# One diffusion-backbone step on one core: branch B projected into turned queries and keys, expert outputs gathered plainly and added by VectorE

## The chip, the core and the metric

The kernel runs on one core of a Trainium2 chip. The metric is the device time of one execution in microseconds (us). The engines are TensorE (PE in the profile; its weight loads PEld), VectorE (DVE), ScalarE (ACT), GpSimd (POOL) and SyncE (SP), which only issues transfers. A trailing q (ACTq) is an engine's queue: issues, loads of registers, waits.

## The reference

Two layers run over 640 tokens of width 1024: 512 latent tokens and 128 context tokens, all in f32. Per layer:

```
mod = silu(cond) @ w_mod + b_mod                # shift, scale, gate, twice
h   = x * (1 + sc1) + sh1
qa,ka,va, qb,kb,vb, qc,kc,vc = split(h @ w_in)  # branches A, B, C
y   = (ga*(oa@w_br0) + gb*(ob@w_br1) + gc*(oc@w_br2)) @ w_o
x   = layernorm(alpha*x + g1*y)
m   = top-2 of 16 experts on x*(1+sc2)+sh2, each (silu(h@w1)*(h@w3))@w2
x   = layernorm(alpha*x + g2*m)
```

Branch A is differential attention with rotary positions, B is neighbourhood attention (8 heads, no rotary positions and no norm of queries and keys, window bias), C is grouped-query attention with normed queries and keys. Latent tokens also read cached context keys and values. The context tokens' new keys and values are outputs too.

## The kernel before, in words

Tokens lie in five tiles of 128 (`NT = 5`, the last is the context). The weights are one wall of 1 MB pieces in device memory; SyncE streams them in order into a ring of six slots (`load`, L602) and waits for a slot to be freed by TensorE or VectorE. Each f32 matmul is two instructions on TensorE in the trace.

Each layer is one block, with a program for each engine. It goes through the branches A, B, C: `project(br)`, `attend(br)`, `merge(br)`. `PU` lists the projection's units: (branch, chunk of 512 columns of `w_in`, token tile). A unit is eight matmuls with `hT` (the modulated input, features on partitions) as the stationary operand and 512 columns of the ring as the moving one (L808, through the helper `mm`), into one of four PSUM banks. ScalarE copies the unit to `tok` (L1371); TensorE turns it, four transposes against the identity one unit later (`transpose_unit`, L883); ScalarE copies the result into `QT` (scaled, L1335) or `KT` (L1337). This holds for branch B's query and key chunks 3 and 4 also, ten units. Chunk 5 holds B's values and is not turned. In branch B's projections VectorE sums sixteen modulation pieces from the ring (L1660, L1662); TensorE adds them over the partitions at the places that `MOD_SUMS` names, behind unit (4, 0) and unit (5, 3) (`sum_partials`, L835). GpSimd stores new keys from `tok` and waits for the store, then the values, and prepares B's bias.

Gates of the merge are computed by `fill`: units of eight matmuls with the ring's weights as the stationary operand and 320 columns of `hT` as the moving one. Eight of these matmuls stand ahead of the last transposes of branch A, the rest between the parts of the attention.

The experts: for each of 17 blocks of 128 tokens GpSimd gathers token rows (`gather`, L742), TensorE turns them and multiplies with w1, w3, w2. ScalarE takes the latent gate row times a flag (`slot_gate`, L559); VectorE, once w2's result is ready, adds the context part (L563) and multiplies the result by the token's weight and the gate row (L564). Both are in `gate_output`, called by `keep_output`. ScalarE stores the block's rows (L1487). At the end of the layer's block ScalarE waits for its stores. Then every engine loads a count (L2018), meets the others at a barrier (L2019), and the next block begins.

```
for t in range(4):
    fetch_outputs(pool, t)      # two gathers a tile: L537 adds into x, L538 writes Y2
scale_power(pool, ch, 0)
fetch_outputs(pool, 4)
```

`fetch_and_scale` runs on GpSimd at the start of layer 1 and in the final block. The first gather accumulates in the transfer (`compute_op=ALU.add`) into `x`, which already holds the scaled residual. VectorE adds `Y2` and takes statistics (`add_outputs`, L551, L494 to L499), GpSimd raises the variance to the power -0.5 (`scale_power`, L504), VectorE makes the negated mean (L1528), ScalarE normalises (L1299) and TensorE turns the tile (L853). The final block does the same with sums (L2141, L2142), squares by ScalarE (L2129), variance (L2147), centring times the gain (L2151) and scaling plus offset (L2153); SyncE loads gain and offset rows `rowsF` (1 MB) at the start of this block and stores each finished tile.

## Time and profile before

| what | us |
|---|---|
| median of 3 runs (lowest, highest) | 2271.79 (2268.26, 2272.42) |
| the profiled execution | 2269.82 |
| its span, first to last instruction | 2267.7 |
| TensorE busy | 2115.3 |
| VectorE busy | 1083.0 |
| ScalarE, GpSimd busy | 519.6, 236.7 |

The mean granted clock of TensorE is 0.971 of full speed. Busy time is not the bound by itself: what matters is who waits at each place. In a timeline a row gives start, duration, engine, line, operation, output and inputs, the count of merged instructions, and in brackets the idle time before it with what ended it. Matmuls are pipelined and their ends modelled: the pace of a run is read from the start of a row to the start of the next one.

### The profile page before, as it was taken

Reading aid. Unit: us, or ns where it says so; the run is one execution under the profiler, and the core shown is the slowest. Engines: PE = TensorE matmul, PEld = TensorE weight load, DVE = VectorE, ACT = ScalarE, POOL = GpSimd, SP = SyncE. Lnnn points to the kernel's source line nnn. Section 1 sums busy time; section 2 is a strip of 40 time slices with the busy share of each in tenths; the row PEclk is TensorE's granted clock in tenths of the full one; section 3 lists DMA queues with packets and bytes.
Section 4 is the critical chain, followed back from the end, with each engine's and each line's share of the span. In section 5 each row is a group of like instructions: output and inputs, shape, how many; then the busy total and the mean of one; then the engine's idle time right before and its main releaser. Section 6 shows DMA issues by size and latency. Waiting matters only on the chain. (4 is left out here: it accounts for less than half of the span.)

```text
span 2267.7 us, 26885 instructions
## 1 busy us (share of the span) xinstructions
PE 2115.3 (93%) x10730; PEld 1376.2 (61%) x10730; DVE 1083.0 (48%) x1701; ACT 519.6 (23%) x992; POOL 236.7 (10%) x272
## 2 busy tenths in 40 slices
PE   6999999999999998899689999999999999969991
PEld 3457754576567654788544676447756775458880
DVE  1135457243444364664242453745434444865434
ACT  2014301242134200122130341113402440012221
POOL 1000010020100000211110001002101000011113
PEclk8999999999999999899899999999999999979996
DMA  8121166311110325899760111642111105159985
GB/s 335 44 78 38 48 217 227 112 52 60 56 40 32 159 104 222 293 370 359 259 221 37 61 38 61 223 172 82 45 60 58 38 20 232 40 188 361 362 323 176
DMA packets 59439, 334.64 MB, mean 148 GB/s; under 512 B 8704, under 2 KB 9696, under 8 KB 30192
## 3 DMA queue, kind: packets, MB, share of 16 engines
q1 hardware_dynamic: 33408, 238.70, 29.0%
q0 software_dynamic: 15008, 56.96, 7.6%
q10 hardware_dynamic: 10896, 37.23, 4.2%
q8 instruction: 87, 1.43, 0.3%
q14 instruction: 40, 0.33, 0.0%
HBM read 300.47 MB, written 35.01 MB: 148 GB/s over the span
## 5 line engine op out<-in xcount | busy, mean ns | idle before, releaser
L808 PE MATMUL ps<-ring,hT 128*128 128x512 f32 (+1 forms) x1280 | 530.5, 570 | 1.9 <-issue 1.9
L808 PE MATMUL ps<-hT,ring 128*128 128x320 f32 x1536 | 464.3, 440 | 0.0
L808 PEld LDWEIGHTS ps<-ring,hT 128*128 128x128 f32 x1280 | 239.8, 191 | 253.6 <-issue 246.8
L808 PEld LDWEIGHTS ps<-hT,ring 128*128 128x128 f32 x1536 | 272.8, 190 | 97.3 <-issue 1.6
L808 PEld LDWEIGHTS ps<-zT,ring 128*128 128x128 f32 x2176 | 254.1, 194 | 18.4 <-issue 15.3
L808 PE MATMUL ps<-zT,ring 128*128 128x128 f32 x2176 | 258.5, 278 | 2.3 <-ACT zT L1483 2.3
L808 PE MATMUL ps<-R,ring 128*128 128x512 f32 (+1 forms) x768 | 211.1, 435 | 4.6 <-DVE zT L1795 3.2
L1430 ACT COPY R<-ps 128x512 f32<-128x512 f32 (+2 forms) x170 | 96.2, 566 | 383.8 <-PE ps L1021 381.6
L808 PEld LDWEIGHTS ps<-R,ring 128*128 128x128 f32 x768 | 116.9, 191 | 98.6 <-issue 92.5
L808 PE MATMUL ps<-ring,zT 128*128 128x512 f32 x320 | 139.0, 593 | 0.0
L1662 DVE SCALAR_TENSOR_TENSOR R<-ring,cs,R 128x2048 f32<-128x2048 f32 x56 | 131.7, 2352 | 5.8 <-DMA ring<-in_wall 4.0
L960 PE MATMUL ps<-R 64*128 64x128 f32 (+2 forms) x992 | 123.2, 374 | 7.0 <-ACT R L1337 3.5
L808 PE MATMUL ps<-ring,R 128*128 128x512 f32 x272 | 122.5, 593 | 3.1 <-issue 3.1
L1725 DVE RECIPROCAL rinv<-rsum 128x2 f32<-128x2 f32 x96 | 15.9, 166 | 218.4 <-ACT R L1416 218.4
L960 PEld LDWEIGHTS ps<-R 64*128 64x128 f32 x992 | 92.1, 186 | 37.9 <-issue 12.2
L563 DVE SCALAR_TENSOR_TENSOR R<-R 128x1024 f32<-128x1024 f32 x34 | 43.7, 1285 | 142.8 <-PE ps L808 142.8
L1695 DVE TENSOR_REDUCE nmax<-ps 128x2 f32<-128x1280 f32 x64 | 95.5, 1492 | 28.6 <-PE ps L960 27.8
L808 PEld LDWEIGHTS ps<-ring,zT 128*128 128x128 f32 x320 | 60.2, 190 | 72.7 <-issue 72.2
L1416 ACT ACTIVATE R<-ps,nmax 128x640 f32<-128x640 f32 x128 | 100.5, 790 | 2.5 <-DVE nmax L1695 0.5
L1371 ACT COPY R<-ps 128x512 f32<-128x512 f32 (+1 forms) x54 | 28.5, 527 | 309.4 <-PE ps L808 309.0
L1021 PEld LDWEIGHTS ps<-ident,R 128*128 128x128 f32 x648 | 76.9, 141 | 29.0 <-DVE R L1716 6.3
L1021 PE MATMUL ps<-ident,R 128*128 128x128 f32 x648 | 87.8, 273 | 6.1 <-DVE R L1716 4.3
(237 smaller groups left out, 1954.2 us busy)
## 6 DMA issues: line engine op xcount, KB each, us to landing
ring<-in_wall SPq DMA_DIRECT2D x224, 1024.0 KB
y_rows<-R ACTq DMA_DIRECT2D x34, 512.0 KB, 9.6
R<-in_rows POOLq DMA_DIRECT2D x2, 4096.0 KB, 15.3
R<-mrows POOLq DMA_DIRECT2D x16, 512.0 KB, 17.8
R<-in_x ACTq DMA_DIRECT2D x10, 512.0 KB, 8.5
h_rows<-R ACTq DMA_DIRECT2D x10, 512.0 KB, 2.7
R<-in_bias POOLq DMA_DIRECT2D x8, 384.0 KB, 4.1
x_state<-R POOLq DMA_DIRECT2D x1, 2560.0 KB, 9.8
```

The source lines that it names most:

```text
L563: ch.step(nc.vector.scalar_tensor_tensor(gsel[e % 2], G2[:, 1, :], in_ctx[:, 0, e:e + 1], gsel[e % 2], ALU.mult, ALU.add), v_chain)
L808: ins = nc.tensor.matmul(out, w, m, start=start, stop=stop, **kw)
L960: return nc.tensor.matmul(out, QT[lo:lo + 64, b, 128 * r:128 * r + 128], KT[lo:lo + 64, key_slot(br, b), k0:k0 + n], start=True, stop=True)
L1021: last = nc.tensor.transpose(ps[:, 3 + c + k // 4, 128 * (k % 4):128 * (k % 4) + 128], P[:, i % 2, c, 128 * k:128 * k + 128], ident[:])
L1371: ch.step(nc.scalar.copy(dst, src), a_copy)
L1416: ins = nc.scalar.activation(dst, src, ACT.Exp, bias=nmax[:, n + a:n + a + 1], accum_out=rsum[:, n + a:n + a + 1])
L1430: ch.step(nc.scalar.copy(dst, src), a_pt)
L1662: ins = V_.scalar_tensor_tensor(mod_acc[:, v], w, c, mod_acc[:, v], ALU.mult, ALU.add)
L1695: ch.step(V_.tensor_reduce(nmax[:, n:n + 2].unsqueeze(2), src, axis=AX.X, op=ALU.max, negate=True), v_max)
L1725: ch.step(V_.reciprocal(rinv[:, o:o + 2], rsum[:, n:n + 2]), v_rinv)
```

## The change

- Chunks 3 and 4 (queries and keys of branch B) are projected turned: eight units each instead of five (`turned`, `units`), with a 128-column slice of the ring as the stationary operand and 320 tokens of `hT` as the moving one. ScalarE copies the unit right into `QT` (scaled) or `KT`. Their transposes and second copies are gone; `QU` and `NEW_K` leave them out. The new keys are stored from `KT`, and the host turns the array. ScalarE waits for that store ahead of branch C. `MOD_SUMS` has (4, 1) for (4, 0).
- `gate_output` is split into `slot_gates` (L563's product, now ahead of the wait for w2's result) and `keep_gated`.
- `y_out` is cleared no more between blocks and counts over both layers (`stores`). ScalarE doesn't wait for the stores at the end of the block; GpSimd does, ahead of the gathers. Spare expert blocks use `extra_out`.
- Both outputs of a token are gathered plainly, into `Y1` and `Y2`; VectorE adds `Y1` (`first_outputs`).
- `rowsF` lies elsewhere and is loaded behind the last layer's weights. The final block sums two tiles ahead of the scaling.

```diff
@@ -53,7 +53,7 @@
 MOD_ORDER = ((2, 6, 0), (0, 0, 8))
-MOD_SUMS = ((4, 0), (5, 3))
+MOD_SUMS = ((4, 1), (5, 3))
 PROJECT_SLOTS = (0, 1, 2, 3, 4, 5) + 3 * (2, 3) + (0, 1) + 4 * (2, 3)
@@ -150,6 +150,11 @@
+def stores(layer, e, n):
+    return layer * len(range(n, NB, 2)) + len(range(n, e, 2))
 def near_values(r):
@@ -160,6 +165,16 @@
     return [*range(LAT), 5]
+def turned(c):
+    return c in (3, 4)
+def units(c):
+    return 8 if turned(c) else NT
@@ -292,11 +307,12 @@
+        Y1 = zf.rearrange("p (t n) -> p t n", t=NT)
         Y2 = area(8704, 5120).rearrange("p (t n) -> p t n", t=NT)
-        rowsF = area(0, 2048).rearrange("p (a n) -> p a n", a=2)
+        rowsF = area(24064, 2048).rearrange("p (a n) -> p a n", a=2)
@@ -308,6 +324,8 @@
         y_init = ctx.enter_context(nc.semaphore("output_rows_filled"))
+        y_out = [ctx.enter_context(nc.semaphore(f"expert_outputs_stored_{n}")) for n in range(2)]
+        last_rows_in = ctx.enter_context(nc.semaphore("last_rows_loaded"))
         full = [sem(f"piece_loaded_{s}") for s in range(SLOTS)]
@@ -533,12 +552,14 @@
-            first, second = (bass.IndirectOffsetOnAxis(ap=yrow[:, k, t:t + 1], axis=0) for k in range(2))
-            pool.indirect_dma_start(out=x[:, t, :], out_offset=None, in_=y_all, in_offset=first, compute_op=ALU.add).then_inc(yt_in[t], 16)
-            pool.indirect_dma_start(out=Y2[:, t, :], out_offset=None, in_=y_all, in_offset=second).then_inc(yt_in[t], 16)
-        def fetch_and_scale(pool, ch):
+            for k, Y in enumerate((Y1, Y2)):
+                pool.indirect_dma_start(out=Y[:, t, :], out_offset=None, in_=y_all,
+                                        in_offset=bass.IndirectOffsetOnAxis(ap=yrow[:, k, t:t + 1], axis=0)).then_inc(yt_in[t], 16)
+        def fetch_and_scale(pool, ch, layer):
+            for n in range(2):
+                pool.wait_ge(y_out[n], 16 * stores(layer, NB, n))
             for t in range(4):
@@ -546,6 +567,11 @@
+        def first_outputs(dve, ch, t):
+            dve.wait_ge(yt_in[t], 32)
+            ch.step(nc.vector.tensor_tensor(x[:, t, :], x[:, t, :], Y1[:, t, :], ALU.add), v_chain)
         def add_outputs(ch, t):
@@ -558,9 +584,12 @@
-        def gate_output(ch, e, w, s):
+        def slot_gates(ch, e):
             ch.step(nc.vector.scalar_tensor_tensor(gsel[e % 2], G2[:, 1, :], in_ctx[:, 0, e:e + 1], gsel[e % 2], ALU.mult, ALU.add), v_chain)
+        def keep_gated(ch, e, w, s):
             ch.step(nc.vector.scalar_tensor_tensor(ysb[:, e % 2, :], flat(4, 1024), w, gsel[e % 2], ALU.mult, ALU.mult), s)
@@ -614,6 +643,8 @@
                         load(i, layer, first + (MOE0 + n))
+                    if last_layer:
+                        sp.dma_start(rowsF[:], A["last_rows"]).then_inc(last_rows_in, 16)
                     if not last_layer:
@@ -688,7 +719,12 @@
                             typ = CHUNK_TYPE[c]
-                            if typ in ("k", "kv"):
+                            if typ == "k" and turned(c):
+                                pool.wait_ge(a_copy, AU.index(PU.index((br, c, units(c) - 1))) + 1)
+                                pool.dma_start(OUT["bk"][layer].rearrange("p (b t) -> p b t", b=4), KT[:, :, LTOK:TOK]).then_inc(new_k_out, 16)
+                                pool.wait_ge(new_k_out, 16 * (br + 1))
+                            elif typ in ("k", "kv"):
@@ -915,6 +951,11 @@
                                         wk = take("in").rearrange("p (k n) -> p k n", k=8)[:, k, :]
+                                    if turned(c):
+                                        b, part = divmod(t, 2)
+                                        last = mm(ps[:, bank_of(i), 0:320], wk[:, 128 * b:128 * b + 128], hT[:, k, 320 * part:320 * part + 320],
+                                                  k == 0, k == KB - 1, frees=k < KB - 1)
+                                        continue
                                     last = mm(ps[:, bank_of(i), 0:w], hT[:, k, 128 * t:128 * t + 128], wk, k == 0, k == KB - 1, frees=k < KB - 1)
@@ -963,7 +1004,7 @@
-                            pe.wait_ge(a_qk, 10 * (br + 1))
+                            pe.wait_ge(a_qk, 20 if br == 2 else 10)
                             pe.wait_ge(a_copy, len([a for a in AU if PU[a][0] <= br]))
@@ -1337,8 +1378,10 @@
                     def project(br):
+                        if br == 2:
+                            act.wait_ge(new_k_out, 32)
                         for c in CHUNKS[br]:
-                            for t in range(NT):
+                            for t in range(units(c)):
                                 i = PU.index((br, c, t))
@@ -1358,6 +1401,9 @@
                                         pass
+                                    elif turned(c):
+                                        b, part = divmod(t, 2)
+                                        dst, src = (QT if c == 3 else KT)[:, b, 320 * part:320 * part + 320], ps[:, bank_of(i), 0:320]
                                     elif CHUNK_TYPE[c] in ("v", "kv"):
@@ -1367,7 +1413,9 @@
                                         dst, src = tok[:, q % 2, :], ps[:, bank_of(i), :]
-                                    if c != 6:
+                                    if c == 3:
+                                        ch.step(nc.scalar.activation(dst, src, ACT.Copy, scale=HD ** -0.5), a_copy)
+                                    elif c != 6:
                                         ch.step(nc.scalar.copy(dst, src), a_copy)
@@ -1501,8 +1549,6 @@
                     store_output(NB - 1)
-                    for s in range(2):
-                        act.wait_ge(y_out[s], 16 * len(range(s, NB, 2)))
@@ -1558,10 +1604,11 @@
                         for t in range(NT + 1):
+                            if t < NT:
+                                first_outputs(dve, ch, t)
                             if t:
                             if t < NT:
-                                dve.wait_ge(yt_in[t], 32)
                                 add_outputs(ch, t)
@@ -1981,10 +2028,11 @@
                         dve.wait_ge(a_gsel, e + 1)
+                        slot_gates(ch, e)
                         dve.wait_ge(pe_e, e + 1)
-                        if e >= 2:
-                            dve.wait_ge(y_out[e % 2], 16 * (e // 2))
-                        gate_output(ch, e, slot_w[:, e, e:e + 1] if e < NE else extra_w[:, NE:NE + 1], v_y)
+                        if stores(layer, e, e % 2):
+                            dve.wait_ge(y_out[e % 2], 16 * stores(layer, e, e % 2))
+                        keep_gated(ch, e, slot_w[:, e, e:e + 1] if e < NE else extra_w[:, NE:NE + 1], v_y)
@@ -2137,7 +2186,7 @@
-                    dve.wait_ge(yt_in[t], 32)
+                    first_outputs(dve, ch, t)
                     ch.step(nc.vector.scalar_tensor_tensor(x[:, t, :], x[:, t, :], 1.0, Y2[:, t, :], ALU.mult, ALU.add, accum_out=lnst[:, t, 12:13]), v_chain)
@@ -2146,20 +2195,25 @@
+                def centred(t):
+                    ch.step(nc.vector.scalar_tensor_tensor(x[:, t, :], x[:, t, :], lnst[:, t, 14:15], rowsF[:, 0, :], ALU.add, ALU.mult), v_chain)
                 def scaled(t):
-                    ch.step(nc.vector.scalar_tensor_tensor(x[:, t, :], x[:, t, :], lnst[:, t, 14:15], rowsF[:, 0, :], ALU.add, ALU.mult), v_chain)
                     dve.wait_ge(g_rs, t + 1)
-                dve.wait_ge(rows_in, 16)
+                dve.wait_ge(last_rows_in, 16)
+                summed(0)
                 for t in range(NT):
-                    summed(t)
-                    if t:
-                        variance(t - 1)
-                        scaled(t - 1)
-                variance(NT - 1)
-                scaled(NT - 1)
+                    if t == 0:
+                        summed(1)
+                    variance(t)
+                    centred(t)
+                    if t + 2 < NT:
+                        summed(t + 2)
+                    scaled(t)
```

## Rows read from the trace of the kernel before

**Rows 1.** The page: busy time, share of the span, instructions.
```profile
PE 2115.3 (93%) x10730; PEld 1376.2 (61%) x10730; DVE 1083.0 (48%) x1701; ACT 519.6 (23%) x992; POOL 236.7 (10%) x272
```

**Rows 2.** Timeline, PE, projections of branch B, layer 0: start us, us, what.
```profile
340.90 7.03 PE L808 MATMUL ps<-ring,hT 128*128 128x512 f32 x16
347.77 0.60 PE L883 MATMUL ps<-ident,R 128*128 128x128 f32 x4
348.20 7.03 PE L808 MATMUL ps<-ring,hT 128*128 128x512 f32 x16
...
414.79 1.92 PE L835 MATMUL ps<-R 128*32 128x512 f32 x16
```

**Rows 3.** Timeline, PE: 320-column matmuls ahead of and inside the attention.
```profile
1253.73 4.47 PE L808 MATMUL ps<-hT,ring 128*128 128x320 f32 x16
1258.04 0.60 PE L883 MATMUL ps<-ident,R 128*128 128x128 f32 x4
...
426.95 3.50 PE L808 MATMUL ps<-hT,ring 128*128 128x320 f32 x12
430.38 0.92 PE L960 MATMUL ps<-R 64*128 64x256 f32 x8
```

**Rows 4.** Timeline, DVE: its last modulation sums, layer 0.
```profile
391.97 4.74 DVE L1662 SCALAR_TENSOR_TENSOR R<-ring,cs,R 128x2048 f32<-128x2048 f32 x2 [0.33 <-DMA ring<-in_wall]
```

**Rows 5.** Timeline, end of layer 0's experts: VectorE and ScalarE's queue.
```profile
1116.46 1.29 DVE L563 SCALAR_TENSOR_TENSOR R<-R 128x1024 f32<-128x1024 f32 x1 [3.58 <-PE ps L808]
...
1119.16 0.34 ACTq L1487 DMA_DIRECT2D y_rows<-R  x1
```

**Rows 6.** Line L2018, GpSimd's queue: duration ns, first and last start.
```profile
L2018 POOLq TENSOR_LOAD <-ovi x2: 320/410/499, 1122.2 to 2225.4; - x2
```

**Rows 7.** Busy time by windows: the engines, granted clock, DMA share, GB/s.
```profile
1120.00:1121.00 1.00, 0.00 (x0) 0.00 (x0) 0.00 (x0) 0.00 (x0) 0.00 (x0) 1.00 1.03 422
...
1132.00:1133.00 1.00, 0.00 (x0) 0.00 (x0) 0.00 (x0) 0.00 (x0) 0.69 (x2) 0.50 0.99 188
```

**Rows 8.** Timeline, POOL: gathers of tile 0 ahead of layer 1.
```profile
1124.74 1.58 POOL L537 DMA_INDIRECT R<-y_rows,yrow  x1 [35.26 <-issue]
1126.63 0.98 POOL L538 DMA_INDIRECT R<-y_rows,yrow  x1 [0.30 <-issue]
```

**Rows 9.** Line L538, the second outputs' gathers: issue to landing.
```profile
DMA to landing us min/median/max: 6.6/8.3/9.5
```

**Rows 10.** Line L742, the experts' token gathers: issue to landing.
```profile
DMA to landing us min/median/max: 5.7/8.9/9.8
```

**Rows 11.** Timeline, all engines: tile 0 ahead of layer 1.
```profile
1133.35 1.23 DVE L551 TENSOR_TENSOR R<-R 128x1024 f32<-128x1024 f32 x1 [7.02 <-DMA R<-y_rows,yrow]
...
1136.31 0.15 DVE L499 TENSOR_SCALAR small<-R 128x1 f32<-128x1 f32 x1
1137.29 0.59 POOL L504 TENSOR_TENSOR R<-small,half 128x1 f32<-128x1 f32 x1
...
1139.59 1.97 PE L853 MATMUL ps<-ident,R 128*128 128x128 f32 x8 [23.34 <-ACT R L1299]
```

**Rows 12.** Timeline, all engines: the final block.
```profile
2227.83 1.58 POOL L537 DMA_INDIRECT R<-y_rows,yrow  x1 [35.14 <-PEq L2107]
...
2237.52 1.23 DVE L2141 SCALAR_TENSOR_TENSOR R<-R 128x1024 f32<-128x1024 f32 x1 [15.24 <-DMA R<-y_rows,yrow]
...
2244.89 2.60 POOL L537 DMA_INDIRECT R<-y_rows,yrow  x1 [0.28 <-POOL R L504]
...
2253.63 1.57 POOL L504 TENSOR_TENSOR R<-small,half 128x1 f32<-128x1 f32 x1 [3.18 <-DVE small L2147]
...
2255.30 1.28 DVE L2153 SCALAR_TENSOR_TENSOR R<-R 128x1024 f32<-128x1024 f32 x1 [0.51 <-POOL R L504]
...
2260.06 1.28 DVE L2153 SCALAR_TENSOR_TENSOR R<-R 128x1024 f32<-128x1024 f32 x1 [0.51 <-POOL R L504]
...
2263.36 1.28 DVE L2153 SCALAR_TENSOR_TENSOR R<-R 128x1024 f32<-128x1024 f32 x1 [0.51 <-POOL R L504]
```

More of the change, by code:

```diff
@@ L376, in count @@
                 return self.n.get(s.num, 0)
-        PU = [(br, c, t) for br in range(3) for c in CHUNKS[br] for t in range(NT)]
+        PU = [(br, c, t) for br in range(3) for c in CHUNKS[br] for t in range(units(c))]
         def bank_of(i):
@@ L387, in out_bank @@
             return (i + 2) % 4
-        QU = [i for i, (br, c, t) in enumerate(PU) if CHUNK_TYPE[c] != "v"]
+        QU = [i for i, (br, c, t) in enumerate(PU) if CHUNK_TYPE[c] != "v" and not turned(c)]
         def by_dve(c, t):
@@ L402, in follows @@
             return i > 0 and i - 1 in QU and PU[i - 1][0] == br and i + 1 < len(PU)
-        NEW_K = [i for i, (br, c, t) in enumerate(PU) if t == CTX and CHUNK_TYPE[c] in ("k", "kv")]
+        NEW_K = [i for i, (br, c, t) in enumerate(PU) if t == CTX and CHUNK_TYPE[c] in ("k", "kv") and not turned(c)]
         def item(br, i):
@@ L637, in _ @@
                         pool.wait_ge(y_init, 16 * len(range(1, EXTRA, 4)))
-                        fetch_and_scale(pool, ch)
+                        fetch_and_scale(pool, ch, layer - 1)
                     def powers(dst, src):
@@ L698, in _ @@
                                 if typ == "k":
-                                    pool.dma_start(OUT[("ak", "bk")[br]][layer], tok[:, q % 2, 0:512]).then_inc(new_k_out, 16)
+                                    pool.dma_start(OUT["ak"][layer], tok[:, q % 2, 0:512]).then_inc(new_k_out, 16)
                                 else:
@@ L1339, in project @@
                     def project(br):
+                        if br == 2:
+                            act.wait_ge(new_k_out, 32)
                         for c in CHUNKS[br]:
-                            for t in range(NT):
+                            for t in range(units(c)):
                                 i = PU.index((br, c, t))
@@ L2078, in _ @@
                             act.wait_ge(v_y, 1)
[L2079 to L2080 removed]
+                            act.dma_start(A["y_rows"][NE + j], ysb[:, 0, :]).then_inc(extra_out, 16)
+                            act.wait_ge(extra_out, 16)
                         @block.vector
@@ L2099, in _ @@
                             dve.wait_ge(a_gsel, 1)
+                            slot_gates(ch, NE)
                             dve.wait_ge(pe_e, 1)
-                            gate_output(ch, NE, extra_w[:, NE:NE + 1], v_y)
+                            dve.wait_ge(y_out[NE % 2], 16 * stores(layer, NB, NE % 2))
+                            keep_gated(ch, NE, extra_w[:, NE:NE + 1], v_y)
                     nc.all_engine_barrier(sems_to_clear=all_sems)
@@ L2118, in _ @@
                 ch = Chain(pool)
-                fetch_and_scale(pool, ch)
+                fetch_and_scale(pool, ch, DEPTH - 1)
                 pool.dma_reset(all_sems)
```

8 lines of the change are left out of this document (3 added, 5 removed).

## The prediction

> **What bounds the kernel now.** I read the page first: TensorE is busy 93% of a span of 2267.7 us [rows 1]. So either its own work gets shorter or one of its pauses does; elsewhere nothing counts. Then TensorE's timeline through the projections of branch B, where the first part of the change lies. A unit is 16 instructions (8 f32 matmuls, two instructions each): they start at 340.90, the next instruction at 347.77, so a unit of 512 columns takes 6.87 us; the four transposes of the unit before take 0.43 us more, until 348.20 [rows 2]. No row there carries an idle time: the engine is the bound of this stage. VectorE sums the modulation pieces beside it and is done at 396.71, 18 us before TensorE asks for that sum at 414.79 [rows 2, 4].
>
> The second kind of place is where TensorE has nothing to do: between the last expert of layer 0 and layer 1 it is idle for 23.34 us, until 1139.59 [rows 11], and behind the last expert of layer 1 for good. In both pauses there is one chain: VectorE gates the last expert's output, ScalarE stores it, the block ends, GpSimd gathers, VectorE normalises. I read it in the timelines of these stretches [rows 5, 8, 11, 12].
>
> **Turned queries and keys.** Per layer, two chunks of 5 units go (10 x 6.87 = 68.7 us) and their 10 groups of transposes (10 x 0.43 = 4.3 us): 73.0 us. In come 2 x 8 units of 8 matmuls with 320 columns. The trace has just this unit in the fill behind branch A: 16 instructions from 1253.73 to 1258.04, 4.31 us [rows 3]. 16 x 4.31 = 69.0 us, so 4.1 us less per layer, 8.2 us in both. The columns are the same 5120; what is saved is the transposes. The upper bound of the price is the run of 12 such instructions between score tiles: 426.95 to 430.38, 3.43 us, 0.572 us per matmul [rows 3]. 128 x 0.572 = 73.2 us would give 0.2 us per layer back instead. I take 4.31, since its neighbours are 128-row work, as the new units' are; the 12 stand beside 64-row score tiles. ScalarE copies 16 times 320 columns in place of 20 times 512, so less than before: nothing. VectorE's first sum is now asked for behind 10 units of 4.31 (43.1 us from the chunk's start) instead of 6 x 6.87 + 5 x 0.43 (43.4 us): no new wait. The second comes 4.1 us sooner, against the 18 us of slack. The store of new keys moves to rows of the turned tile and GpSimd waits for it as before, one chunk ahead of anything due; nothing, by that cover. If the store were late, the next late thing would be the value store and the bias of the second head pair behind it in GpSimd's queue.
>
> **The last expert's gate.** The product of gate rows now stands ahead of the wait for TensorE. VectorE was idle for 3.58 us when it started at 1116.46, 1.29 us long [rows 5]. So the last store is issued 1.3 us sooner, at both ends. In the other experts TensorE does not wait for this: nothing.
>
> **The store's wait.** ScalarE issues the last store at 1119.16, and every engine gets past the block's end only at 1122.2 (its first instruction there is the load at L2018); the data moves from 1120 on, at full share of the engines that carry it [rows 5, 6, 7]. The first gather comes at 1124.74, 2.5 us behind L2018 [rows 8]. Now ScalarE leaves right behind its issue: 1119.16 + 0.34 - 1.30 = 1118.20, with an estimated 0.25 us for the block's end 1118.45, and the gathers could start at 1121.0. The store itself has landed by 1122.2 - 1.3 = 1120.9 at the latest, so GpSimd's new wait is over at about the same time. Gathers start 3.7 us sooner, of which 1.3 is the gate; the same at the end, where L2018 starts at 2225.4 and the gather at 2227.83 [rows 6, 12]. Bounds: 1.3 (the end of the block hangs on something else) and 3.7.
>
> **Gathers and adds, between the layers.** An accumulating gather occupies GpSimd 1.58 us, a plain one 0.98, each with 0.30 behind it [rows 8]. Tile 0's second gather starts 1.89 us behind the first and lands 6.6 later [rows 8, 9], 8.5 us from the start; VectorE begins at 1133.35, 8.61 us from it [rows 11]. The engines that move the data are at full share with only 188 GB/s while the accumulating ones run, against 422 GB/s in the store [rows 7]: they are the slow part. Plain gathers of the same size, from the token rows, land in 5.7 us at least [rows 10]. So tile 0 is in at 1.28 + 5.7 = 7.0 us, 1.6 us less. Then VectorE adds for 1.26 us more. This leaves 0.35 us. But its order changes too: the next tile's first add now stands ahead of the negated mean, and it has two operands in SBUF. The rows show what that does: a small power takes 0.59 us with VectorE on other work, 1.57 beside such an instruction [rows 11, 12]; a gather issue 2.60 instead of 1.58 [rows 8, 12]. I carry it through: the second add and the statistics took 3.11 us (1133.35 to 1136.46), so tile 0 has them at 7.0 + 1.26 + 3.11 = 11.4; the power is held until the next add ends at 12.65 and is done 0.4 later (in the end it was done at 2255.20, that far behind the instruction that held it, an estimate); from the power's end to TensorE's start it is 1139.59 - 1137.88 = 1.7 us, so TensorE comes in at 14.75 [rows 11, 12]. Before: 1139.59 - 1124.74 = 14.85. Gain of this part 0.1 us, I count 0. Bounds: 1.1 gained (nothing held), 1.1 lost (landing no sooner). Later tiles are covered by TensorE's work on the tile before, over the 6.87 us of its unit, by my estimate with 1 us to spare; without it each would cost the add's 1.26.
>
> [...]
>
> **Gathers and adds at the end.** Before, from the first gather to the last result: 2264.64 - 2227.83 = 36.8 us [rows 12]. VectorE's period per tile is 2260.06 - 2255.30 = 4.76 us, of which it waits 0.51 for GpSimd's power [rows 12]. The new order puts tile t+2's sum behind the power, so this wait goes from all but the last two tiles; the first add comes in with 1.26. Busy: 4.25 + 1.26 = 5.51 per tile. New: landing 7.0 (before 9.7, when VectorE began at 2237.52, since the two last rows' 1 MB moved beside it; now it is loaded during the experts) + 5 x 5.51 + 0.9 = 35.4 us. Gain 1.4 us. Tile 4's gathers are issued behind the first power, each held by VectorE as above; they land at about 23 us, VectorE asks at 23.7. Bounds: 3 gained, 0.5 lost.
>
> **Sum.** 8.2 + 3.7 + 0 + 3.7 + 1.4 = 17.0 us. The profiled execution took 2269.82 us, so 2252.8. It lies 2.0 under the median of the runs, 2271.79, so against the median I forecast 2254.8 us.
>
> **The rivals.** About 4.5 us (0.2%) is what a measurement here can tell from no change.
> - Turned units at the pace of the score stage (0.565 to 0.572 us per matmul). For it: every 320-column run in the attention has this pace. Against: each run of 16 has 4.31. Gain 17.0 - 8 = 9: 2262.8. Chance 13%.
> - The adds eat more: gathers of later tiles are each held by VectorE's two-operand adds, about 1.1 us each for two gathers at either place, and tile 4 comes 1.5 us late at the end. 17.0 - 3.7 = 13.3: 2258.5. For it: the 2.60 row. Against: most gathers are issued before VectorE starts. 17%. [...]
> - The wait has only moved: GpSimd waits for the store as long as ScalarE did. Only the gate's 1.3 is left at each place: 17.0 - 4.8 = 12.2: 2259.6. 8%.
> - The change doesn't do what it says: the turned stage becomes bound by the modulation sums or their loads, and the ends give back their part: within 0.2%. For it only that VectorE is busy until 396.71. 4%.
> - Slower: in the turned stage the ring is the stationary operand while VectorE reads the same ring and loads arrive at the same time; no 128-row run shows that. The price is 2 x 128 x (p - 0.539) us. It eats the 17.0 at p = 0.605 and is slower by over 0.2% from 0.623. Its time at 0.64, an estimate further out than any row, is 2280.6. Against: the slowest row has 0.572. 3%.
> - More than forecast (gathers landing sooner, nothing held): 2251 or less, 5%.
>
> **Numbers.** My forecast has 50%, from 2251.5 to 2258. The range goes from 2249 to 2263: below, all bounds of the ends at their best; above, up to the first rival. Faster by over 0.2%: 0.93, within: 0.04, slower: 0.03.
>
> **What would show it.** Right: units of 4.31 us in the projections of branch B with no transposes among them, and the first score tile 4.1 us sooner against the stage's start; VectorE's gate rows ahead of the last expert's matmuls; L2018's counterpart less than 1 us behind the last store's issue; tile 0 landing about 7 us behind the first gather; the last result 35 us behind it. Wrong: a turned unit over 4.5 us, idle time of TensorE before either modulation sum, a first gather that waits over 0.5 us for the store, or a VectorE that waits for tile 2 or 4 at the end.

## The result and the profile after

The change takes **2255.61 us** (median of 6 runs, 2253.59 to 2257.16), the kernel before beside it 2270.29 us (2267.14 to 2272.43): a ratio of **0.9935**, 95% interval 0.9923 to 0.9948. That is 14.7 us less; forecast were 17.0 less, 2254.8 us, in the range of 2249 to 2263. The profiled execution of the change took 2254.81 us, its span is 2252.8; against the profiled one of before, 2269.82, that is 15.0 us less.

The page's busy line, against [rows 1]:

```profile
PE 2108.4 (94%) x10842; PEld 1407.1 (62%) x10842; DVE 1094.8 (49%) x1711; ACT 509.4 (23%) x984; POOL 230.1 (10%) x272
```

TensorE is busy for 93.6% of the shorter span, before for 93.3%. For the parts, I take the stages one by one. TensorE's timeline through the projections of branch B of layer 0 (start and length in us, engine, line, operation; a group's length reaches from its first start to its last end), against [rows 2]:

```profile
312.43 43.23 PE L844 MATMUL ps<-hT,ring 128*128 128x320 f32 x160
355.59 1.92 PE L871 MATMUL ps<-R 128*32 128x512 f32 x16
...
410.95 1.92 PE L871 MATMUL ps<-R 128*32 128x512 f32 x16
...
422.02 1.16 PE L1001 MATMUL ps<-R 64*128 64x128 f32 x16
```

160 instructions are 10 turned units: 355.59 - 312.43 = 43.16 us, 4.316 us each, forecast 4.31. There are no transposes among them, and no bracket with an idle time at either modulation sum (L871). From the stage's start to the first score tile (L1001) it takes 109.59 us; the kernel before takes 113.74 (312.12 to 425.86), and so does the kernel with this part undone, below.

The timeline around the place between the layers, against [rows 5, 8, 11]:

```profile
1107.56 1.28 DVE L589 SCALAR_TENSOR_TENSOR R<-R 128x1024 f32<-128x1024 f32 x1 [0.28 <-ACT R L585]
...
1110.74 1.28 DVE L593 SCALAR_TENSOR_TENSOR R<-ps,R 128x1024 f32<-128x1024 f32 x1 [1.90 <-PE ps L844]
1112.12 0.34 ACTq L1535 DMA_DIRECT2D y_rows<-R  x1
1115.73 0.29 DVE L1562 TENSOR_TENSOR R<-par 128x128 f32<-128x128 f32 x1 [3.70 <-PEq L2067]
...
1116.07 0.94 POOL L556 DMA_INDIRECT zT<-y_rows,yrow  x1 [33.66 <-issue]
...
1122.63 1.22 DVE L573 TENSOR_TENSOR R<-R,zT 128x1024 f32<-128x1024 f32 x1 [5.06 <-DMA R<-y_rows,yrow]
...
1127.04 1.22 DVE L573 TENSOR_TENSOR R<-R,zT 128x1024 f32<-128x1024 f32 x1
1127.09 1.61 POOL L523 TENSOR_TENSOR R<-small,half 128x1 f32<-128x1 f32 x1 [1.16 <-DVE small L518]
1128.80 0.21 DVE L1574 TENSOR_SCALAR R<-R 128x1 f32<-128x1 f32 x1 [0.54 <-POOL R L523]
...
1130.41 1.97 PE L889 MATMUL ps<-ident,R 128*128 128x128 f32 x8 [19.77 <-ACT R L1340]
```

L589 (the gate rows) is done while TensorE still works for the last expert, and only L593 waits for TensorE. The first gather begins 3.95 us behind the issue of the store, before it was 5.58 [rows 5, 8]. How VectorE holds GpSimd is to be seen in the last lines: the second L573 (tile 1's first add) starts at 1127.04, the power of tile 0 at 1127.09 and takes 1.61 us, so the negated mean (L1574) starts only when the add is over. TensorE's pause is 19.77 us, against 23.34 [rows 11].

The same at the end, against [rows 12]:

```profile
2210.02 0.34 ACTq L1535 DMA_DIRECT2D y_rows<-R  x1
2213.77 0.94 POOL L556 DMA_INDIRECT zT<-y_rows,yrow  x1 [33.46 <-PEq L2157]
...
2220.74 1.23 DVE L573 TENSOR_TENSOR R<-R,zT 128x1024 f32<-128x1024 f32 x1 [10.81 <-DMA R<-y_rows,yrow]
...
2223.84 1.23 DVE L573 TENSOR_TENSOR R<-R,zT 128x1024 f32<-128x1024 f32 x1 [0.41 <-DMA R<-y_rows,yrow]
...
2248.46 1.28 DVE L2205 SCALAR_TENSOR_TENSOR R<-R 128x1024 f32<-128x1024 f32 x1 [0.51 <-POOL R L523]
```

Tile 0 is in 6.97 us behind the first gather (forecast 7.0); the last result is done at 2249.74, 35.97 us behind it (forecast 35.4, before 36.81). VectorE waits 0.41 us for tile 1's gathers and 0.51 for each of the last two powers.

A table of both timelines, each step from its first to its last event, in us:

| step | before | after | gained | forecast |
|---|---|---|---|---|
| turned queries and keys, layer 0 (score start, less the stage's start) | 113.74 | 109.59 | 4.15 | 4.1 |
| the same, layer 1 | 113.74 | 109.59 | 4.15 | 4.1 |
| last expert's tanh to its gated output, between the layers | 7.96 | 6.52 | 1.44 | 1.3 |
| the same, at the end | 7.95 | 6.52 | 1.43 | 1.3 |
| store's issue to first gather, between the layers | 5.58 | 3.95 | 1.63 | 2.4 |
| the same, at the end | 5.47 | 3.75 | 1.72 | 2.4 |
| first gather to TensorE, between the layers | 14.85 | 14.34 | 0.51 | 0 |
| first gather to last result, at the end | 36.81 | 35.97 | 0.84 | 1.4 |

The gains sum to 15.9 us. Stages that the change doesn't touch were 0.9 us longer in the changed kernel's execution: the projections of layer 0's branch B began 0.3 us later, TensorE waited 1.14 us in place of 0.79 for VectorE in layer 1's last merge, and the routing stages (router power to first expert) took 0.2 us more in both together. That leaves the 15.0 us. That wait is 0.79 us in some of the kernels below and 1.14 in others, with and without turned units. In the second routing stage, gather to first tanh took 19.10 and 17.67 us in two profiled executions of the changed kernel. So a single execution can be 1.5 us longer or shorter by that stage alone, and I judge the single runs below by their segments.

### The profile page after: what moved, and what is told of

Its sections match the earlier page's. It is cut to its first block and busy times, and to the rows that moved or that the text cites. A ratio compares the mean times of both kernels' runs of the same rounds, so it can differ in the third digit from the quotient of the medians.

```text
span 2252.8 us, 27060 instructions
## 1 busy us (share of the span) xinstructions
PE 2108.4 (94%) x10842; PEld 1407.1 (62%) x10842; DVE 1094.8 (49%) x1711; ACT 509.4 (23%) x984; POOL 230.1 (10%) x272
## 3 DMA queue, kind: packets, MB, share of 16 engines
q8 instruction: 87, 1.43, 0.3%
## 5 line engine op out<-in xcount | busy, mean ns | idle before, releaser
L844 PE MATMUL ps<-hT,ring 128*128 128x320 f32 x2048 | 603.0, 438 | 0.0
L844 PEld LDWEIGHTS ps<-hT,ring 128*128 128x128 f32 x2048 | 369.7, 190 | 138.9 <-issue 3.3
L844 PE MATMUL ps<-ring,hT 128*128 128x512 f32 (+1 forms) x960 | 390.1, 562 | 1.9 <-issue 1.9
L844 PEld LDWEIGHTS ps<-ring,hT 128*128 128x128 f32 x960 | 180.8, 192 | 185.6 <-issue 178.5
L1001 PE MATMUL ps<-R 64*128 64x128 f32 (+2 forms) x992 | 123.2, 374 | 7.1 <-ACT R L1378 3.6
L1772 DVE RECIPROCAL rinv<-rsum 128x2 f32<-128x2 f32 x96 | 15.9, 166 | 218.3 <-ACT R L1464 218.3
L1001 PEld LDWEIGHTS ps<-R 64*128 64x128 f32 x992 | 92.1, 186 | 38.1 <-issue 12.2
L593 DVE SCALAR_TENSOR_TENSOR R<-ps,R 128x1024 f32<-128x1024 f32 x34 | 43.6, 1284 | 91.1 <-PE ps L844 91.1
L844 PEld LDWEIGHTS ps<-ring,R 128*128 128x128 f32 x272 | 49.0, 190 | 52.2 <-issue 52.2
```

What stands on the lines that cost most here:

```text
L593: ch.step(nc.vector.scalar_tensor_tensor(ysb[:, e % 2, :], flat(4, 1024), w, gsel[e % 2], ALU.mult, ALU.mult), s)
L844: ins = nc.tensor.matmul(out, w, m, start=start, stop=stop, **kw)
L1001: return nc.tensor.matmul(out, QT[lo:lo + 64, b, 128 * r:128 * r + 128], KT[lo:lo + 64, key_slot(br, b), k0:k0 + n], start=True, stop=True)
L1772: ch.step(V_.reciprocal(rinv[:, o:o + 2], rsum[:, n:n + 2]), v_rinv)
```

## Experiments

All are the changed kernel with one thing altered. **The turned stage undone:**

```diff
-    return c in (3, 4)
+    return False
-MOD_SUMS = ((4, 1), (5, 3))
+MOD_SUMS = ((4, 0), (5, 3))
...
-pe.wait_ge(a_qk, 20 if br == 2 else 10)
+pe.wait_ge(a_qk, 10 * (br + 1))
```

> The changed kernel with branch B's queries and keys projected as before (five units of 512 columns per chunk, transposes and second copies back); all else stays changed. Theory (the parts add up, the turned units give 4.15 us per layer): 8.3 us more than the changed kernel, so about 2264 us against 2255.6, and in the timeline units of 6.87 us with 0.43 us of transposes between. Rival (the ends react to where the stage finishes, or the turned units only moved a wait): under 5 us or over 11 us more.

Measured: 2264.73 us (2262.19 to 2265.99), ratio to the kernel before 0.9970 (0.9960 to 0.9981). Its median is 9.1 us over the change's, 6.0 under that of the kernel before; by the two ratios it is 7.9 us over the change. Its TensorE timeline:

```profile
311.31 13.90 PE L844 MATMUL ps<-ring,hT 128*128 128x512 f32 x32
325.04 0.60 PE L919 MATMUL ps<-ident,R 128*128 128x128 f32 x4
325.48 7.03 PE L844 MATMUL ps<-ring,hT 128*128 128x512 f32 x16
332.35 0.60 PE L919 MATMUL ps<-ident,R 128*128 128x128 f32 x4
...
425.05 1.16 PE L1001 MATMUL ps<-R 64*128 64x128 f32 x16
```

332.35 - 325.48 is the unit of 6.87 us, 325.48 - 325.04 the 0.44 us of transposes. The stage is 4.15 us longer than in the change, 8.3 us for two layers. The turned stage holds over half of the gain, and the rival that had its matmuls at 0.572 us is out: 16 units at that pace would have taken 0.2 us a layer more than the old ones.

The edit as shown is the core; the store of the new keys goes back to its old rows with it.

**The last expert's gate behind the wait again:**

```diff
-                        slot_gates(ch, e)
                         dve.wait_ge(pe_e, e + 1)
+                        slot_gates(ch, e)
```

> The changed kernel with the gate rows' product behind the wait for w2's result again. Theory: only the last expert counts; from the last hidden activation of ScalarE to the last gated output it is 7.95 us at both layers' ends instead of 6.52, so 1.4 us twice; the experts keep their period of 11.66 us. 2258.5 us. Rival: the product was hidden under the block's end anyway, 0 us, or the experts' period grows.

Measured, one run: 2255.35 us. The timeline:

```profile
1106.99 0.38 ACT L1547 ACTIVATE R<-ps 128x256 f32<-128x256 f32 x1 [8.63 <-PE ps L844]
...
1112.28 1.28 DVE L589 SCALAR_TENSOR_TENSOR R<-R 128x1024 f32<-128x1024 f32 x1 [3.51 <-PE ps L844]
1113.60 1.28 DVE L593 SCALAR_TENSOR_TENSOR R<-ps,R 128x1024 f32<-128x1024 f32 x1
```

From tanh to gated output 7.89 us instead of 6.52, at both places: 1.37 us each. The total of this one execution doesn't show the 2.7 us; it lies within the change's own runs. What follows is from the segment: the gate gives what its instruction lasts, and nothing in the other experts, whose period is 11.66 us in both kernels.

**ScalarE waits for its stores again before it leaves the block:**

```diff
                     store_output(NB - 1)
+                    for s in range(2):
+                        act.wait_ge(y_out[s], 16 * stores(layer, NB, s))
```

> The changed kernel with ScalarE waiting for the stores at the end of the block again (GpSimd's wait stays too). Theory: from the last store's issue to the first gather it is 5.5 us instead of 3.95 and 3.75. The loads of the count at the block's end, which take ScalarE 1.05 us in the changed kernel, take 0.46 us again as before, because they then run behind the store and not beside it: the 0.6 us that the removed wait gave less than forecast. Rival: the loads are slow for another reason (1.05 us stays) and the store's landing is what gathers wait for. 2259 us.

Measured, one run: 2259.27 us. From the store's issue to the first gather 5.66 and 5.52 us, in the change 3.95 and 3.75: 1.71 and 1.77 us each. The forecast had 2.4. Where the rest went is in the load of the counter that each engine takes at the block's end. Of this kernel (operation and tile, count, shortest, median and longest in ns, first and last start in us):

```profile
L2068 POOLq TENSOR_LOAD <-ovi x2: 313/403/493, 1116.9 to 2215.6; - x2
L2068 ACTq TENSOR_LOAD <-ovi x2: 457/466/475, 1117.0 to 2215.6; - x2
L2068 DVEq TENSOR_LOAD <-ovi x2: 312/431/550, 1117.0 to 2215.7; - x2
```

and of the change, against [rows 6]:

```profile
L2066 POOLq TENSOR_LOAD <-ovi x2: 606/844/1082, 1112.8 to 2210.7; - x2
L2066 ACTq TENSOR_LOAD <-ovi x2: 1046/1052/1058, 1112.9 to 2210.8; - x2
L2066 DVEq TENSOR_LOAD <-ovi x2: 814/986/1158, 1112.9 to 2210.8; - x2
```

With the wait, the load comes when the store's data have moved (share of the engines that carry them 0.06 from 1116.0 to 1116.5, then 0.00; the load starts at 1116.9 to 1117.0), and takes ScalarE 466 ns. Without it, the load starts 0.7 us behind the store's issue, beside its transfer (418 GB/s from 1113.5 to 1114.0), and takes 1052 ns. Behind it every engine meets the others at the barrier, and the longest load of any is 1158 ns in place of 550: about 0.6 us are given back at each place. The first gather starts 0.34 us behind VectorE's first instruction in the change (1116.07, 1115.73) and 0.35 in this kernel (1119.57, 1119.22), where no data had moved from 1116.5 on, against 0.26 in the kernel before, where GpSimd has no such wait: its own wait for the stores costs under 0.1 us.

**Only the first gather accumulates again, all else as in the change.** This is the comparison that the forecast never made: it held the kernel before against the change, in which order, loads and gathers differ together.

```diff
-                pool.indirect_dma_start(out=Y1[:, t, :], ..., in_=y_all, ...)
+                pool.indirect_dma_start(out=x[:, t, :], ..., in_=y_all, ..., compute_op=ALU.add)
...
-            ch.step(nc.vector.tensor_tensor(x[:, t, :], x[:, t, :], Y1[:, t, :], ALU.add), v_chain)
```

> The changed kernel with the first output of each token accumulated into x by the transfer again and no add by VectorE; stores' wait, order of the final block and turned units stay changed. Theory A (VectorE's add pays since the accumulating transfers are the slow part): tile 0 lands 8.5 us behind the first gather instead of 6.9, layer 1's TensorE starts 14.8 us behind it (14.3 with the plain gathers), the last result comes 37 us or more behind the final block's first gather (36.0), since tiles 2 to 4 land late; 2257 us. Theory B (in the final block VectorE's adds are the bound and the transfers have time): a tile's period falls from 5.54 to about 4.3 us and the last result comes 33 to 34 us behind the first gather, so the plain gathers lose there what the new order would give; 2253 us.

> The kernel in which every first gather accumulates, as before the change, and all else is as in the change, once more beside the sorted kernel for a common measure. Its segments in its first profile were 15.00 us (first gather to TensorE, between the layers) and 35.55 us (first gather to last result). If its 2253.4 us there was its own and not the spread, it comes to 0.992 of the kernel before again; by the segments alone it is 0.2 us slower than the change, 0.9935.

Measured: 2253.41 us (2252.64 to 2254.90), ratio 0.9923 (0.9909 to 0.9937), and again 2254.48 us (2252.53 to 2255.65), ratio 0.9925 (0.9911 to 0.9938). Timeline of the first, at the end:

```profile
2212.71 1.58 POOL L556 DMA_INDIRECT R<-y_rows,yrow  x1 [33.48 <-PEq L2156]
...
2221.33 1.23 DVE L2189 SCALAR_TENSOR_TENSOR R<-R 128x1024 f32<-128x1024 f32 x1 [12.49 <-DMA R<-y_rows,yrow]
...
2225.78 1.23 DVE L2189 SCALAR_TENSOR_TENSOR R<-R 128x1024 f32<-128x1024 f32 x1 [3.03 <-DMA R<-y_rows,yrow]
...
2246.98 1.28 DVE L2204 SCALAR_TENSOR_TENSOR R<-R 128x1024 f32<-128x1024 f32 x1 [0.51 <-POOL R L523]
```

VectorE starts 8.62 us behind the first gather, 1.65 later than with plain gathers, and waits 3.03 for tile 1, 2.62 more than with them: the transfers bound its first tiles. It also waits for tiles 2 and 4, 0.69 and 0.87 us (0.67 and 1.66 in the second profile), where the change has no wait. Against these 5.8 us it has five adds of 1.26 us less to do, 6.3 us, and the last result comes 35.55 us behind the gather (36.30 in the second profile); in the change it is 35.97, and 35.65 in a second profile. Between the layers: 15.00 and 14.75 us from gather to TensorE, in the change 14.34 and 14.41. So the plain gathers with adds are worth 0.5 us between the layers and nothing that two profiles each can show at the end. The end came at neither of the values that the theories had (33 to 34 us, or 37 and more), since the waits that the plain gathers save and the adds that they cost cancel almost to nothing. The medians of the runs lie on the accumulating kernel's side, by 1.1 to 3.1 us; the intervals of the ratios overlap, and no segment of the traces holds those microseconds. That stays open.

This kernel also shows what no run undoes by itself, the earlier load of the gain and offset rows. It gathers as the kernel before does, and VectorE starts 8.62 us behind the first gather at the end instead of 9.69 [rows 12]: 1.07 sooner, and as soon as between the layers (8.61), where no such rows are loaded. At tile 1 0.35 of it is left (13.07 us instead of 13.42).

**The negated mean ahead of the next tile's first add,** between the layers:

```diff
-                            if t < NT:
-                                first_outputs(dve, ch, t)
                             if t:
                                 negated_mean(t - 1)
                             if t < NT:
+                                first_outputs(dve, ch, t)
                                 add_outputs(ch, t)
```

> The change, with the negated mean of the tile before ahead of the next tile's first add on VectorE between the layers. Theory A (the power of tile 0 and the negated mean are held by the add, as the forecast carried it through): the power of tile 0 takes 0.6 us instead of 1.61, the negated mean follows it at once, and TensorE starts about 1.0 us sooner behind the first gather, 13.3 us instead of 14.34. Theory B (the power is slow for another reason, such as gathers on GpSimd beside it): it still takes 1.6 us and the start stays at 14.3 us. The end of the kernel is not touched: 35.97 us from the first gather to the last result, within 0.1 us.

Measured, one run: 2251.72 us. The timeline:

```profile
1115.97 0.94 POOL L556 DMA_INDIRECT zT<-y_rows,yrow  x1 [33.65 <-issue]
...
1126.86 0.57 POOL L523 TENSOR_TENSOR R<-small,half 128x1 f32<-128x1 f32 x1 [1.16 <-DVE small L518]
1127.54 0.21 DVE L1574 TENSOR_SCALAR R<-R 128x1 f32<-128x1 f32 x1 [0.77 <-POOL R L523]
...
1129.14 1.97 PE L889 MATMUL ps<-ident,R 128*128 128x128 f32 x8 [18.60 <-ACT R L1340]
```

The power takes 0.57 us, and TensorE starts 13.17 us behind the gather, 1.2 sooner than in the change. Of the 1.61 us that this power took in the change, 1.04 was VectorE's add. The end, not touched, took 35.83 us.

TensorE's start is not all that counts here. After the pause its granted clock is 0.50, and 1.00 comes back at another time in each execution. Two stretches of 0.5 us, of the change and of this kernel (busy us of PE, PEld, DVE, ACT and POOL with the count of instructions, the granted clock, the share of the engines that move data, and GB/s):

```profile
1135.41:1135.91 0.50, 0.50 (x2) 0.20 (x1) 0.43 (x3) 0.07 (x1) 0.00 (x0) 0.69 0.00 0
```

```profile
1132.14:1132.64 0.50, 0.50 (x2) 0.17 (x2) 0.43 (x3) 0.15 (x1) 0.40 (x1) 0.80 0.93 344
```

In the change the clock rises about 5.3 us behind TensorE's start, here about 3.2, in the two kernels below that have the same order about 6.2. So TensorE comes to tile 1's transposes 6.84 us behind its start here, 7.89 in the change (7.71 in its second profile), 8.3 in those two. From the first gather to these transposes it is 20.01 us here, 22.23 and 22.12 in the change, 21.98 and 21.69 in those two: with that order TensorE starts 0.7 to 1.2 us sooner, and is 0.1 to 2.2 us ahead one tile later. What sets the moment of the rise no run here shows; part of this run's low total is that moment, and not the order.

**The final block's old order, with plain gathers:**

```diff
-                summed(0)
                 for t in range(NT):
-                    if t == 0:
-                        summed(1)
-                    variance(t)
-                    centred(t)
-                    if t + 2 < NT:
-                        summed(t + 2)
-                    scaled(t)
+                    summed(t)
+                    if t:
+                        variance(t - 1)
+                        centred(t - 1)
+                        scaled(t - 1)
```

> The change, with plain gathers, but the final block's order of before on VectorE (sum of a tile, then the tile before it finished), so that the wait for GpSimd's power stands in each tile again. Theory A (the forecast's: the reordering pays for the adds): a period of about 6.0 us in place of 5.54, and the last result 37.5 to 38 us behind the first gather instead of 35.97. Theory B (GpSimd's power isn't waited for any more with plain gathers): a period of 5.5 us and 36 us as in the change.

Measured, one run: 2257.25 us. The timeline at the end:

```profile
2214.76 0.94 POOL L556 DMA_INDIRECT zT<-y_rows,yrow  x1 [33.45 <-PEq L2157]
...
2235.41 1.28 DVE L2205 SCALAR_TENSOR_TENSOR R<-R 128x1024 f32<-128x1024 f32 x1 [0.53 <-POOL R L523]
...
2241.42 1.28 DVE L2205 SCALAR_TENSOR_TENSOR R<-R 128x1024 f32<-128x1024 f32 x1 [0.51 <-POOL R L523]
...
2250.73 1.29 DVE L2205 SCALAR_TENSOR_TENSOR R<-R 128x1024 f32<-128x1024 f32 x1 [0.51 <-POOL R L523]
```

The period is 6.01 us instead of 5.54, with 0.51 of waiting for the power in each, and the last result comes 37.26 us behind the gather, 1.3 later than in the change. Plain gathers in the old order would have made the end 0.45 us slower than it was [rows 12], and that with the gain and offset rows loaded earlier: there the new order is what carries the adds.

**Both kinds of gather, by place.** First tiles 0 and 1 plain with adds and tiles 2 to 4 accumulated, at both places, with the mean first; beside it the change once more:

```diff
+                if k == 0 and t >= PLAIN:
+                    ... indirect_dma_start(out=x[:, t, :], ..., compute_op=ALU.add)
+                else:
+                    ... indirect_dma_start(out=(Y1, Y2)[k][:, t, :], ...)
```

> The change, with the two kinds of gather mixed: tiles 0 and 1 plain with the add on VectorE, tiles 2 to 4 accumulated into the tokens without an add; and the negated mean ahead of the first add between the layers. Theory A (the accumulating gather costs only what lands first; the later ones are covered): TensorE starts 13.3 us behind the first gather between the layers, and the last result 33 to 34 us behind it at the end (5 x 4.25 + 2 x 1.26 + 7.0 + waits of 2 to 3), together 2.5 to 3.5 us under the change, so 2252 to 2253 us, about as the kernel in which all gathers accumulate or 1 us under it. Theory B (accumulating gathers of tiles 2 to 4 take the transfers' rate and arrive late): VectorE waits over 2 us for tile 2 or 3 at the end, the last result comes 35 us or more behind the first gather, and the time is within 1 us of the change's.

> The change itself once more, on the same chip beside the mixed kernel and in as many rounds, so that the two and the kernel before have one common measure. All theories: 0.9930 to 0.9940 of the kernel before, 2254 to 2256 us.

Measured: 2253.41 us (2251.83 to 2255.07), ratio 0.9919 (0.9904 to 0.9933); the change 2256.55 us (2252.70 to 2257.76), ratio 0.9932 (0.9918 to 0.9946). The last result comes 34.20 us behind the gather, TensorE between the layers 13.66. Theory A gave 33 to 34 and 13.3, theory B 35 and more with a wait over 2 us: A holds, and both of its numbers were a little low. What is late at the end is one tile:

```profile
2229.17 2.23 POOL L559 DMA_INDIRECT R<-y_rows,yrow  x1 [0.28 <-POOL R L524]
...
2238.80 1.22 DVE L2195 SCALAR_TENSOR_TENSOR R<-R 128x1024 f32<-128x1024 f32 x1 [1.55 <-DMA R<-y_rows,yrow]
```

Tile 4's accumulating gather stands behind the first power and is itself held to 2.23 us; VectorE waits 1.55 us for it.

So the next kernel issues tile 4's gathers ahead of that power at the end, and takes plain gathers alone between the layers, where only tile 0 is on the path:

```diff
-            for t in range(4):
+            for t in range(NT if last else 4):
                 fetch_outputs(pool, t, plain)
             scale_power(pool, ch, 0)
-            fetch_outputs(pool, 4)
+            if not last:
+                fetch_outputs(pool, 4, plain)
```

> The change with each place given its own gathers: between the layers all plain, with the negated mean ahead of the next tile's first add; at the end tiles 0 and 1 plain with the add on VectorE, tiles 2 to 4 accumulated, and tile 4's gathers ahead of the first power, which VectorE asks for only behind tile 2's sum. Theory A (tile 4 was late in the mixed kernel only since its gathers stood behind the power): TensorE starts 13.2 us behind the first gather between the layers, as in the kernel with the mean first; at the end VectorE waits under 0.3 us for tile 4 and under 0.6 us for the power of tile 0, and the last result comes 33 to 33.5 us behind the first gather instead of 34.20 in the mixed kernel and 35.97 in the change. Total some 3.7 us under the change: 0.9915 of the kernel before. Theory B (the accumulating gathers are bound by their transfers, not by when they are issued): tile 4 still comes 1 us or more late and the power is late besides, so 34.2 us or more.

Measured: **2249.56 us** (2247.22 to 2250.47), ratio 0.9903 (0.9887 to 0.9918). The accumulating kernel measured beside it took 2254.48 (2252.53 at least), and the change has never been under 2252.70 in 11 runs: this kernel beats both. Its timeline at the end:

```profile
2212.22 0.94 POOL L561 DMA_INDIRECT zT<-y_rows,yrow  x1 [33.44 <-PEq L2165]
...
2226.52 0.72 POOL L524 TENSOR_TENSOR R<-small,half 128x1 f32<-128x1 f32 x1
...
2235.54 1.23 DVE L2198 SCALAR_TENSOR_TENSOR R<-R 128x1024 f32<-128x1024 f32 x1
...
2243.59 1.28 DVE L2213 SCALAR_TENSOR_TENSOR R<-R 128x1024 f32<-128x1024 f32 x1 [0.51 <-POOL R L524]
```

Tile 4's sum (L2198 at 2235.54) has no wait any more, and the first power (0.72 us at 2226.52) is done before VectorE asks for it: theory A, and better than its 33 to 33.5 us; the last result is done at 2244.87, 32.65 us behind the first gather. Between the layers it takes 13.38 us. Against the change that is 3.3 and 1.0 us, 4.3 together (at tile 1's transposes 0.5 of the 1.0 is left); the medians differ by 6.1 to 7.0, more than the segments account for. The runs of the two kernels spread by some 3 to 5 us, and where the rest lies stays open. Tile 4's gathers moved with all gathers plain were not tried, so of the 3.3 us the mixed kernel shows 1.8 for the form of the gathers, and the other 1.5 go with the move.

## Why the prediction was right, and where its terms were off

- **Turned stage, forecast 8.2:** 8.3 from the stage in the two traces and in the undone kernel, 9.1 from the medians, 7.9 from the ratios. The choice of the row with 128-row neighbours over the one beside 64-row score tiles [rows 3] decided this term, and it held: 4.316 us a unit.
- **Gate, forecast 2.6:** 2.9 from the traces, 2.7 from the undone kernel. Right.
- **Store's wait, forecast 4.8:** 3.35 from the traces, 3.5 from the undone kernel. This is the term that was mis-sized, by 0.7 us at each place. The step was to take L2018's counterpart at 0.25 us behind the store's issue, an estimate of mine that no row gives, and all behind it, up to the gather, as it stood. Its place was right within 0.1 us: the load starts at 1112.8, 0.34 us behind the end of the issue. The rest was not as it stood: moved to where the store's transfer still runs (418 GB/s), the same load takes ScalarE 1052 ns in place of 464 in the kernel before. Taking a moved step at its old duration was the error. The rival that GpSimd waits for the store as long as ScalarE did is out by the 0.34 us above.
- **Gathers and adds between the layers, forecast 0:** 0.5 gained. The steps came out nearly as they were carried through: tile 0 in at 6.56 us (7.0), and the power held by the add, 1.61 us. That hold, which the forecast priced, is removable, as the mean-first kernel shows with 1.2 us at TensorE's start.
- **Gathers and adds at the end, forecast 1.4:** 0.84. Tile 0 at 6.97 and a period of 5.54 (5.51) are right; not in the sum were the 0.41 us that VectorE waits for tile 1 and 5 x 0.03. More important is what the term was ascribed to. The forecast called the accumulating gathers "the slow part"; the comparison with only that part put back shows next to nothing at the end (35.55 and 36.30 us against 35.97 and 35.65). The adds are 6.3 us of work on VectorE, and the accumulation costs 5.8 us of waits, 4.3 of them at tiles 0 and 1. Of the 2.7 us by which tile 0 came sooner, 1.07 belong to the gain and offset rows, as the forecast had it, and 1.65 to the plain gathers. The order gives 1.3 us by the old-end kernel. Trading an accumulation for an add in tiles 2 to 4 loses: the mixed kernel takes 1.8 us back, the sorted one, with tile 4's gathers moved too, 3.3. That this term came out near its forecast is in part luck.
- **The sum:** two terms too large (store 1.5, end 0.6), three too small (gate 0.3, between the layers 0.5, turned 0.1), and 0.9 of stages that the change doesn't touch: 15.0 in place of 17.0. The medians, 14.7 apart, say the same. Errors of both signs cancel in part; no term but the store's is off by over 0.6 us.

That a gather's issue is held by VectorE too, which the forecast took from the 2.60 us row [rows 12], holds in the runs: the accumulating issue of tile 4 in the mixed kernel took 2.23 us beside VectorE's two-operand work; the first gather of that kind in [rows 8], beside no such long instruction, 1.58. The last section has more of such rows. On the chain between the layers what was held is tile 0's power (1.61 us), which is no gather. Tile 0's gathers were issued before VectorE began, and the one that was held in that place (tile 3's, 1.13 us in place of 0.94) nobody waited for.

## What to carry to other kernels

When a change swaps one thing and reorders another, price each against the other's new state, not both against the old kernel: the swap here gave 0.5 us at one place and next to nothing at the other, the order 1.3. Choose the form of a transfer by who is late at that tile: the faster transfer for what a pause waits for (here the plain gathers, 406 GB/s; with one of each pair accumulating, 197), the one that saves the busy engine's work for all that lands under cover. And keep the small instruction that GpSimd must do for the critical chain away from VectorE instructions with two operands in SBUF, by putting the consumer of its result ahead of them: here tile 0's power took 1.61 us beside such an add and 0.57 ahead of it.

## What was unexpected of the hardware

- The load of the count at the block's end (TENSOR_LOAD of `ovi`) took every engine longer where the last store's data were still moving. In the change (L2066, from 1112.8 and 2210.7 us on; up to 418 and 410 GB/s in steps of 0.5 us, 0 from 1114.5 and 2212.5 on) it took ScalarE 1046 and 1058 ns, VectorE 814 and 1158, GpSimd 606 and 1082. In the kernel in which ScalarE waits for its stores (L2068, from 1116.9 and 2215.6 us on, 0 GB/s) it took ScalarE 457 and 475 ns, VectorE 312 and 550, GpSimd 313 and 493 (the shorter and the longer of the two loads).
- The issue of a gather of `y_rows` took longer where a VectorE instruction with two operands in SBUF had begun 0.10 us or more before it and had 0.2 us or more left: by what was left, less 0.08 to 0.15 us, at all such places of the profiles. In the old-end kernel 1.12 us were left when it began, and it took 1.98 us instead of 0.94:

```profile
2229.37 1.28 DVE L2205 SCALAR_TENSOR_TENSOR R<-R 128x1024 f32<-128x1024 f32 x1 [0.55 <-POOL R L523]
2229.53 1.98 POOL L556 DMA_INDIRECT zT<-y_rows,yrow  x1 [0.28 <-POOL R L523]
```

In the change 0.73 were left at 2221.24 and it took 1.54; in the mixed kernel 0.76 for an accumulating one, 2.23 instead of 1.57; in the kernel before 1.12, 2.60 instead of 1.58 [rows 12]. Other transfers aren't what held it: from 2229.5 to 2231.5 in the old-end kernel the engines that carry the data were busy for a share of 0.02. And beside the one-operand statistics of the accumulating kernel, with 0.90 us left and those engines at full share, the issue took its usual time:

```profile
1131.26 1.42 DVE L513 BATCH_NORM_STATS2 R<-R 128x6 f32<-128x512 f32 x2
1131.78 0.99 POOL L557 DMA_INDIRECT R<-y_rows,yrow  x1 [0.31 <-issue]
```

Where the GpSimd instruction began 0.04 to 0.06 us behind VectorE's, it went both ways: in the sorted kernel a gather 0.05 us behind (2225.55) took 0.97 us, and in the mean-first kernel a power 0.05 us behind (2229.41) 0.56, while the change's power of tile 0, also 0.05 us behind, took 1.61.
- With the gathers plain, the engines that carry the data moved 406 GB/s at full share; with one of each pair accumulating, 197. A stretch of the change (columns as above):

```profile
1124.00:1128.00 4.00, 0.00 (x0) 0.00 (x0) 3.83 (x6) 0.00 (x0) 2.53 (x3) 0.50 1.00 406
```

and one of the accumulating kernel, with its first gathers under way:

```profile
1118.50:1124.50 6.00, 0.00 (x0) 0.00 (x0) 0.00 (x0) 0.00 (x0) 4.80 (x4) 0.50 1.00 197
```

Both are gathers of the same rows. With half the rate the first tile came 1.65 us later at the end and VectorE waited 3.03 us for the second, and yet the last result came no later than the spread of two profiles.
